# The prompt taken in by pairs of tiles between the weights' loads, and the first norm's squares made from its rows as diagonals

## The chip, the cores and the metric

One NeuronCore of a Trainium2 chip. The metric is device time in microseconds of one execution; given is the median of several runs. PE is the matrix engine (TensorE), ACT the scalar engine, DVE the vector engine, POOL the GpSimd engine, SP the sync engine, which here does nothing but issue DMAs.

## What is computed

One inference step of one decoder layer, for a prompt of 256 tokens and 8 sampled tokens that share the weights, in f32. Cut to what matters here:

```
x = x + 1/2 * SwiGLU_1(RMSNorm(x))       d_model 2048, d_ff 5632
x = x + mixer(RMSNorm(x))                dilated attention and gated linear attention
x = x + 1/2 * SwiGLU_2(RMSNorm(x))
RMSNorm(x) = x * rsqrt(mean(x * x) + 1e-6) * gain
swiglu(h)  = (silu(a) * b) @ w_out,  (a, b) = split(h @ w_in)
```

## The kernel before

**Layout.** `x` lies in SBUF with the features on the partitions: 16 tiles of 128 features x 264 tokens (256 of the prompt, 8 samples). The prompt comes from memory with tokens on the partitions (`xn`, two halves of 128 tokens x 2048 features) and is turned by PE, 128x128 at a time, against the identity matrix `ident` into PSUM (`g0`, `g1`, four banks each, `groups`), from where ACT or DVE copies it to `x`.

**Precision.** Every f32 product is made as three products of rounded parts. Of a chunk of weights (`raw`, 2 row tiles x 512 columns, 512 KB, a ring of 4 slots) ACT makes the high part `wh` (`split`, L1035) and then DVE the low part `wl` (`low`, L1458). In the same way ACT makes `xh` from x times the gain (`x_high_only`, L1051) and DVE makes `xl` (`x_low`, L1492). `multiply` (L592 to L594) issues xh*wh, xl*wh, xh*wl: 24 matmuls of 264 columns for one chunk. DVE's `low` counts `lo_done`, on which SP's next load into the slot and PE wait; PE counts `used`, on which ACT's split of the chunk four later waits.

**The first half-step.** `ffn_in` makes blocks of 512 columns of `w_in`: 8 chunks for the gate (a, in `g0`), 8 for the up part (b, in `g1`). Each engine has its own program, written out by hand, and works it off in order. The norm's factor goes on after the product: beside chunks 0 to 7 the sums of squares are made. ACT squares four tiles of x at a time (L1095), DVE adds these (L1483, L1485) into `ssq`; ahead of chunk 6 PE sums `ssq` over the partitions against ones (`mean`, L603, L604); ACT takes the root after its split of chunk 10 (k = 7, L1056), DVE its reciprocal, and chunk 8 on PE waits for the root.

**What sets the order around the change.** At the start SP issues prompt columns 0 to 511, the sample, columns 512 to 1023, waits for all six gains, and then alternates weights and prompt (`load_x`, `load_first`, L478, L452). ACT issues the loads of `ident` and of the six gains (`gain_rows`) and then waits for the first turned quarter. PE turns the prompt by quarters of four tiles (L664), with the sample (L668) and all gains (L656) between them, all of it before the first product; the third and fourth quarter wait until the banks are copied. Copies alternate: quarters 0 and 2 on ACT (L1090), 1 and 3 on DVE (L1553). Chunks 3 on of the splits are in ACT's `ffn_in` at step k (chunk k + 3), followed by `rest_of_x(k)`; DVE's program has the same steps.

Of the kernel before, what the change touches and what calls it, by code (L numbers as in the profile page):

```python
# [21 lines left out]
F32 = mybir.dt.float32  # L22
# [235 lines left out]
def layer_step(nc, x_prompt, x_sample, cache_k, cache_v, state, g_ffn1, w1_in, w1_out, g_mix, w_in,  # L258
# [5 lines left out]
    with ExitStack() as ctx:  # L264
# [113 lines left out]
        gains_in, gains_full, gains_new = sem("gains_in"), sem("gains_full"), sem("gains_new")  # L378
# [3 lines left out]
        x_in, xs_in = sems("x_in", KT // 4), sem("xs_in")  # L382
        x_turned, xs_turned, xs_new = sem("x_turned"), sem("xs_turned"), sem("xs_new")
        x_even, x_odd = sem("x_even"), sem("x_odd")
# [60 lines left out]
        def _(sp):  # L445
# [29 lines left out]
            def load_x(q):  # L475
                cols = slice(q * CW, (q + 1) * CW)
                src = x_prompt[0, :, cols].rearrange("(h p) d -> p h d", p=P)
                sp.dma_start(xn[:, :, cols], src).then_inc(x_in[q], 16)  # L478
# [102 lines left out]
        def _(pe):  # L581
# [29 lines left out]
            def ffn_in(nth, c0):  # L611
                def body(i, first):
                    for k in range(FI_BODY):
# [3 lines left out]
                        if k == 0 and first:  # L617
                            if nth == 0:
                                pe.wait_ge(x_even, 2)
# [6 lines left out]
                        if k == FI_BODY // 2:  # L626
                            if first:
# [3 lines left out]
                        if first and not up and j % 2 == 0:  # L631
# [16 lines left out]

            pe.wait_ge(ident_in, 16)
            for q in range(KT // 4):  # L650
                if q >= 2:
                    pe.wait_ge((x_even, x_odd)[q % 2], 1)
                if q == 1:
                    pe.wait_ge(gains_in, 16 * 6)
                    n_g = 4 * KT + AT_T + DV // P
                    pe.transpose(g1[:, 3, 0:n_g], gain_rows[0:n_g, :], ident[0:n_g, 0:n_g]).then_inc(gains_full, 1)  # L656
                    pe.wait_ge(gains_new, 1)
                    pe.wait_ge(xs_new, 1)
                pe.wait_ge(x_in[q], 16)
                for n in range(4):  # L660
                    f = slice((4 * q + n) * P, (4 * q + n + 1) * P)
                    g = groups[q % 2]
                    for half in range(2):
                        mm = pe.transpose(g[:, n, half * P:(half + 1) * P], xn[:, half, f], ident[:, :])  # L664
                mm.then_inc(x_turned, 1)
                if q == 0:
                    pe.wait_ge(xs_in, 16)
                    pe.transpose(g1[:, 2, 0:P], xns[:, :], ident[:, :]).then_inc(xs_turned, 1)  # L668
# [356 lines left out]
        def _(act):  # L1025
# [55 lines left out]
            for g in (g_ffn1[0], g_mix[0], g_ffn2[0], g_final, g_att[0], g_gla[0]):  # L1081
                k = g.shape[0] // P
                act.dma_start(gain_rows[n:n + k, :], g.rearrange("(k p) -> k p", p=P)).then_inc(gains_in, 16)
                n += k
            act.wait_ge(gains_new, 1)
            act.wait_ge(eps_set, 1)

            def copy_x(q):
                act.wait_ge(x_turned, q + 1)
                act.activation(x[:, 4 * q:4 * q + 4, 0:TP], groups[q % 2][:, :, 0:TP], ACT.Copy).then_inc(x_even, 1)  # L1090

            def square(q):
                if q:
                    act.wait_ge(sq_part, q)
# [971 lines left out]
```

## Time and profile before

| | us |
|---|---|
| median of 3 runs | 2084.91 (2084.04 to 2087.27) |
| the profiled execution | 2088.0 |
| its span, first to last instruction | 2086.2 |
| PE busy in the span | 2057.1 (99%) |
| DVE, ACT, POOL busy | 1149.4, 893.0, 133.4 |

The span is what the timeline shows; the execution's own time is 1.8 us longer. Times in rows count from the span's start. "Idle before" is the time in which the engine did nothing ahead of a row, with what released it. [...]

### The profile page before, as it was taken

How to read it: one execution, taken by the hardware profiler on the slowest of the kernel's cores; microseconds unless marked ns; L12 is line 12 of the kernel's file. 1: busy time of each engine (PE TensorE's matmuls, PEld its weight loads, DVE VectorE, ACT ScalarE, POOL GpSimd, SP SyncE). 2: the span in 40 equal slices, each digit the busy share in tenths (PEclk: the TensorE clock that was granted, in tenths of full speed). 3: DMA queues.
4: the chain of work that ended last, by engine and by line, in shares of the span. 5: the costliest groups of instructions: out<-in, count | busy, mean ns of one | idle time of the engine just before them, and what ended most of it. 6: DMA issues, size and time to landing. Idle time of an engine off the chain costs nothing.

```text
span 2086.2 us, 40425 instructions
## 1 busy us (share of the span) xinstructions
PE 2057.1 (99%) x16619; PEld 2034.6 (98%) x16619; DVE 1149.4 (55%) x1243; ACT 893.0 (43%) x1050; POOL 133.4 (6%) x161
## 2 busy tenths in 40 slices
PE   8999999999999999999999999999999999999998
PEld 7999999999999999999998899999999999999998
DVE  6555555555444444664578867655555555544443
ACT  6443433444344344444446734444443334433433
POOL 0000000000000001000154750000000000000000
PEclk9999999999999999999999999999999999999999
DMA  6655566656555555447987575566666665565554
GB/s 206 188 178 179 170 187 184 181 177 179 179 181 172 190 177 164 142 127 252 315 279 233 157 228 171 166 195 180 178 180 180 180 181 171 177 188 180 174 180 123
DMA packets 200857, 387.52 MB, mean 186 GB/s; under 512 B 14522, under 2 KB 23428, under 8 KB 200756
## 3 DMA queue, kind: packets, MB, share of 16 engines
q1 hardware_dynamic: 193856, 377.27, 59.2%
q10 hardware_dynamic: 6244, 7.05, 1.0%
q0 software_dynamic: 656, 1.74, 0.2%
q8 instruction: 77, 1.26, 0.2%
q14 instruction: 24, 0.20, 0.0%
HBM read 376.91 MB, written 9.11 MB: 185 GB/s over the span
## 4 chain that ended last, share of the span: by engine, by line
PE 93%; DVE 3%; ACT 1%; DMA 1%; issue 1%; POOL 0%; ACTq 0%; SPq 0%; DVEq 0%
PE g L592 30%; PE g L593 29%; PE g L594 29%; DVE wl L1458 1%; PE g L865 1%; ACT wh L1035 1%; PE g L795 0%; DVE dif L1644 0%; DVE am L1667 0%; DMA bcast<-rows_q 0%; PE g L827 0%; DMA xn<-in_x_prompt_dram 0%; POOL stream L1987 0%; PE g L816 0%; PE g L809 0%
## 5 line engine op out<-in xcount | busy, mean ns | idle before, releaser
L1458 DVE TENSOR_TENSOR wl<-raw,wh 128x1024 fp32r<-128x1024 f32 x658 | 803.3, 1231 | 775.3 <-ACT wh L1035 775.0
L1035 ACT ACTIVATE wh<-raw 128x1024 fp32r<-128x1024 f32 x658 | 689.5, 1055 | 855.0 <-PE g L594 818.4
L592 PE MATMUL g<-xh,wh 128*128 128x264 f32 x3584 | 1028.1, 287 | 5.2 <-DVE va L1611 3.6
L593 PE MATMUL g<-xl,wh 128*128 128x264 f32 x3584 | 1021.2, 285 | 0.0
L594 PE MATMUL g<-xh,wl 128*128 128x264 f32 x3584 | 1020.7, 285 | 0.0
L592 PEld LDWEIGHTS g<-xh,wh 128*128 128x128 f32 x3584 | 678.3, 189 | 10.3 <-issue 8.9
L593 PEld LDWEIGHTS g<-xl,wh 128*128 128x128 f32 x3584 | 677.1, 189 | 0.3
L594 PEld LDWEIGHTS g<-xh,wl 128*128 128x128 f32 x3584 | 675.6, 189 | 0.0
L592 PE MATMUL g<-uh,wh 128*128 128x264 f32 x1408 | 401.0, 285 | 0.0
L593 PE MATMUL g<-ul,wh 128*128 128x264 f32 x1408 | 400.6, 284 | 0.0
L594 PE MATMUL g<-uh,wl 128*128 128x264 f32 x1408 | 400.5, 284 | 0.0
L594 PEld LDWEIGHTS g<-uh,wl 128*128 128x128 f32 x1408 | 265.2, 188 | 0.0
L593 PEld LDWEIGHTS g<-ul,wh 128*128 128x128 f32 x1408 | 265.1, 188 | 0.0
L592 PEld LDWEIGHTS g<-uh,wh 128*128 128x128 f32 x1408 | 264.7, 188 | 0.0
L1074 ACT ACTIVATE uh<-t_buf 128x1056 f32 (+1 forms) x22 | 23.9, 1087 | 102.2 <-DVE t_buf L1531 102.2
L1987 POOL TENSOR_TENSOR stream<-stream,bcast 128x256 f32<-128x256 f32 x64 | 57.0, 926 | 102.4 <-DMA bcast<-rows_q 102.4
L1999 POOL TENSOR_TENSOR stream<-stream,pt_s 128x256 f32<-128x256 f32 x64 | 50.9, 830 | 38.5 <-DMA stream<-in_cache_att_v_dram 19.6
L1958 POOL DMA_DIRECT2D wg<-in_w_gate_dram x1 | 0.5, 513 | 790.6 <-PE g L594 790.6
L1535 DVE TENSOR_TENSOR ul<-t_buf,uh 128x1056 f32 (+1 forms) x22 | 27.7, 1259 | 33.2 <-ACT uh L1074 33.2
L592 PE MATMUL g<-gh,wh 128*128 128x264 f32 x128 | 38.5, 301 | 3.7 <-DVE rg L1611 3.7
L593 PE MATMUL g<-gl,wh 128*128 128x264 f32 x128 | 37.5, 293 | 0.0
L594 PE MATMUL g<-gh,wl 128*128 128x264 f32 x128 | 37.5, 293 | 0.0
(255 smaller groups left out, 1099.5 us busy)
## 6 DMA issues: line engine op xcount, KB each, us to landing
raw<-in_w_ffn_in_dram SPq DMA_DIRECT2D x352, 512.0 KB, 4.5
raw<-in_w_ffn_out_dram SPq DMA_DIRECT2D x176, 512.0 KB, 3.8
raw<-in_w_in_dram SPq DMA_DIRECT2D x96, 512.0 KB, 4.1
raw<-in_w_out_dram SPq DMA_DIRECT2D x32, 512.0 KB, 5.0
stream<-in_state_gla_dram SPq DMA_DIRECT2D x8, 512.0 KB, 7.6
bcast<-rows_v SPq DMA_DIRECT2D x8, 512.0 KB, 8.2
out_dram<-stream ACTq DMA_DIRECT2D x8, 512.0 KB, 7.7
stream<-in_cache_att_k_dram SPq DMA_DIRECT2D x8, 512.0 KB, 6.1
```

What stands on the lines that cost most here:

```text
L592: pe.matmul(out(n), hi, a, start=first and k == 0, stop=False)
L593: pe.matmul(out(n), hi, b, start=False, stop=False)
L594: mm = pe.matmul(out(n), lo, a, start=False, stop=last and k == CK_T - 1)
L865: mm = pe.matmul(held["out"][:, f, b:b + 1], stream[:, (2 * b) % 4, f * P:(f + 1) * P], ones[:, 0, :], start=True, stop=True, skip_group_c ...
L1035: act.activation(dst, src, ACT.Copy).then_inc(hi_done, 1)
L1074: act.activation(uh[:, bass.ds(4 * i, 4), :], t_buf[:, :, :], ACT.Copy).then_inc(uh_new, 1)
L1458: dve.tensor_tensor(dst, src, h.bitcast(F32), ALU.subtract).then_inc(lo_done, 1)
L1535: dve.tensor_tensor(ul[:, bass.ds(4 * i, 4), :], t_buf[:, :, :], uh[:, bass.ds(4 * i, 4), :].bitcast(F32), ALU.subtract).then_inc(ul_new, 1)
L1958: pool.dma_start(wg2[0:RANK, :], w_gate2[0]).then_inc(wg2_in, 16)
L1987: a = pool.tensor_tensor(stream[:, slot, cols], stream[:, slot, cols], bcast[:, b % 2, cols], ALU.mult)
L1999: a = pool.tensor_tensor(v[:, hs, :], v[:, hs, :], pt_s[:, t, hs, b:b + 1].to_broadcast([P, 4, HD]), ALU.mult)
```

## The change

The prompt comes in five loads (two of two tiles, three of four), each between two loads of weights, and the wait for the gains is gone from SP. PE turns it in eight pairs of tiles, all in `g1`: two before the first product, the others ahead of chunks 1, 2 and 4 (`in_front_of`). The copies from PSUM are by pairs (0, 1, 2, 4 and 6 on ACT, 3, 5 and 7 on DVE), and high and low parts are made by pairs. ACT issues a small Copy ahead of all data. The first gains (`gain_in`) are turned alone, the others ahead of chunk 5. The squares are now made from the prompt's rows: ACT squares half a row of tokens (128 tokens x 1024 features) with its accumulator, four times (`square_rows`); DVE adds the two halves and writes them, as a diagonal (`ident` times a column), into `ssq`, makes the sample's squares itself and copies the second gains (`diagonal_squares`, step k = 5).

```diff
+            def load_x(i):
+                cols = slice((0, 2, 4, 8, 12)[i] * P, (2, 4, 8, 12, 16)[i] * P)
...
             load_x(0)
             sp.dma_start(xns[:, :], x_sample[:, 0, :].rearrange("b (k c) -> k b c", c=P)).then_inc(xs_in, 16)
+            load_first(0)
             load_x(1)
-            sp.wait_ge(gains_in, 16 * 6)
-            load_first(0)
+            load_first(1)
             load_x(2)
-            load_first(1)
+            load_first(2)
             load_x(3)
-            load_first(2)
             load_first(3)
+            load_x(4)
...
+                        if first and nth == 0:
+                            in_front_of(k)
+                            if not up:
+                                pe.wait_ge(xl_pair, k + 1)
                         if first and k == 6:
                             if nth == 0:
-                                pe.wait_ge(x_odd, 2)
+                                pe.wait_ge(gains_new, 2)
                             else:
                                 pe.wait_ge(att_taken, FO_BLOCKS)
                             mean(1 + 2 * nth, mean_full)
...
+            def turn_x(pair):
+                pe.wait_ge(x_in[(0, 1, 2, 2, 3, 3, 4, 4)[pair]], 16)
+                if pair >= 4:
+                    pe.wait_ge(x_copied[pair - 4], 1)
+                for i in range(2):
+                    f = slice((2 * pair + i) * P, (2 * pair + i + 1) * P)
+                    for half in range(2):
+                        mm = pe.transpose(g1[:, pair % 4, (2 * i + half) * P:(2 * i + half + 1) * P],
+                                          xn[:, half, f], ident[:, :])
+                mm.then_inc(x_turned, 1)
...
+            turn_x(0)
+            pe.wait_ge(xs_in, 16)
+            pe.transpose(g0[:, 0, 0:P], xns[:, :], ident[:, :]).then_inc(xs_turned, 1)
+            pe.wait_ge(gain_in, 16)
+            pe.transpose(g0[:, 1, 0:KT], gain_rows[0:KT, :], ident[0:KT, 0:KT]).then_inc(gains_full, 1)
+            turn_x(1)
+            pe.wait_ge(xs_new, 1)
+            pe.wait_ge(gains_new, 1)
+
+            def in_front_of(k):
+
+                if k == 1:
+                    turn_x(2)
+                    turn_x(3)
+                elif k == 2:
+                    turn_x(4)
+                    turn_x(5)
+                elif k == 4:
+                    turn_x(6)
+                    turn_x(7)
+                elif k == 5:
+                    pe.wait_ge(gains_in, 16 * 5)
+                    pe.wait_ge(x_copied[4], 1)
...
+            act.wait_ge(eps_set, 1)
+            act.activation(tiny[:, 8:9], eps[:, 0:1], ACT.Copy)
...
+            def square_rows(n):
+                part, half = n // 2, n % 2
+                for i in ((0, 1, 2), (3, 4))[part]:
+                    act.wait_ge(x_in[i], 16)
+                if n:
+                    act.wait_ge(row_sq, n)
+                act.activation(s_buf[:, :, :].rearrange("p n t -> p (n t)")[:, 0:D // 2],
+                               xn[:, half, part * (D // 2):(part + 1) * (D // 2)], ACT.Square,
+                               accum_out=tiny[:, n:n + 1]).then_inc(row_sq, 1)
...
             def rest_of_x(k):
-                if k == 0:
-                    act.wait_ge(x_odd, 2)
-                    x_high_only(3, 0)
-                elif k <= 2:
-                    square(k + 1)
+                if k <= 4:
+                    if k % 2:
+                        copy_x(k + 3)
+                    high_pair(k + 3)
+                    if k:
+                        square_rows(k - 1)
...
+            def diagonal_squares():
+
+                dve.wait_ge(row_sq, 4)
+                link(dve.tensor_tensor(tiny[:, 4:6], tiny[:, 0:2], tiny[:, 2:4], ALU.add))
+                for half in range(2):
+                    dve.tensor_scalar(ssq[:, 0, half * P:(half + 1) * P], ident[:, :], tiny[:, 4 + half:5 + half],
+                                      None, ALU.mult)
...
             def rest_of_x(k):
+                if k <= 4:
+                    if k % 2 == 0:
+                        copy_x(k + 3)
+                    low_pair(k + 3)
+                elif k == 5:
+                    diagonal_squares()
+                    dve.wait_ge(gains_full, 2)
+                    dve.tensor_copy(all_gains[:, KT:], g1[:, 0, KT:4 * KT + AT_T + DV // P]).then_inc(gains_new, 1)
```

PE, around the mean, before (semaphores waited for in brackets; `xl_new`, `xl_pair` are low parts of x):

```order
L593 MATMUL g<-xl,wh 128x264
L594 MATMUL g<-xh,wl 128x264
L603 MATMUL g<-ssq,ones 128x264 [waits consts_in,ssq_new,x_odd]
L604 MATMUL g<-ssq,ones 128x264
L592 MATMUL g<-xh,wh 128x264 [waits lo_done,xl_new]
```

and the same place in the change:

```order
L594 MATMUL g<-xl,wh 128x264
L595 MATMUL g<-xh,wl 128x264
L604 MATMUL g<-ssq,ones 128x264 [waits ssq_new,consts_in,gains_new,xl_pair]
L605 MATMUL g<-ssq,ones 128x264
L593 MATMUL g<-xh,wh 128x264 [waits lo_done]
```

The mean stands where it stood, ahead of chunk 6; it now waits for the second gains (`gains_new`) and the low parts of pair 6 as well.

ACT, from the split of chunk 3 on, before (`used` is PE's count of chunks, `raw_full` a landed load):

```order
L1035 ACTIVATE wh<-raw 128x1024 [waits used,raw_full3]
L1051 ACTIVATE xh<-x,all_gains 128x264 [waits x_odd]
L1051 ACTIVATE xh<-x,all_gains 128x264 x3
L1035 ACTIVATE wh<-raw 128x1024 [waits used,raw_full0]
L1095 ACTIVATE s_buf<-x 128x1056 [waits sq_part]
L1035 ACTIVATE wh<-raw 128x1024 [waits used,raw_full1]
L1095 ACTIVATE s_buf<-x 128x1056 [waits sq_part]
L1035 ACTIVATE wh<-raw 128x1024 [waits used,raw_full2]
```

and the change, from the split of chunk 4 on:

```order
L1057 ACTIVATE wh<-raw 128x1024 [waits used,raw_full0]
L1113 ACTIVATE x<-g 128x2x256 [waits x_turned]
L1120 ACTIVATE xh<-x,all_gains 128x264 [waits x_copied4]
L1120 ACTIVATE xh<-x,all_gains 128x264
L1129 ACTIVATE s_buf,tiny<-xn 128x1024 [waits x_in2,x_in1,x_in0]
L1057 ACTIVATE wh<-raw 128x1024 [waits used,raw_full1]
L1120 ACTIVATE xh<-x,all_gains 128x264 [waits x_copied5]
L1120 ACTIVATE xh<-x,all_gains 128x264
L1129 ACTIVATE s_buf,tiny<-xn 128x1024 [waits x_in2,row_sq,x_in1,x_in0]
L1057 ACTIVATE wh<-raw 128x1024 [waits used,raw_full2]
```

High parts, copies and squares now stand between the splits of chunks 4 to 8, where before there were one pass of squares after chunk 4, one after chunk 5, and nothing after that.

DVE, at the end of that stretch (steps k = 4 and 5), in the change:

```order
L1496 TENSOR_TENSOR wl<-raw,wh 128x1024 [waits hi_done]
L1591 COPY x<-g 128x2x256 [waits x_turned]
L1597 SCALAR_TENSOR_TENSOR xl<-x,all_gains,xh 128x264 [waits xh_pair]
L1597 SCALAR_TENSOR_TENSOR xl<-x,all_gains,xh 128x264
L1496 TENSOR_TENSOR wl<-raw,wh 128x1024 [waits hi_done]
L1604 TENSOR_TENSOR tiny<-tiny 128x2 [waits row_sq]
L1606 TENSOR_SCALAR ssq<-ident,tiny 128x128 [waits vec]
L1606 TENSOR_SCALAR ssq<-ident,tiny 128x128
L1609 TENSOR_TENSOR t_buf<-x 128x128
L1611 TENSOR_REDUCE ssq<-t_buf 128x8 [waits vec]
L1630 COPY all_gains<-g 128x58 [waits gains_full]
```

Before, DVE's additions of squares were done by step k = 2; now `ssq` is written after the low part of chunk 8 (the second row with `wl`), and the copy of the gains comes last.

## Rows read from the trace of the kernel before

**Rows 1.** The page's chain that ended last, by engine, share of the span.
```profile
PE 93%; DVE 3%; ACT 1%; DMA 1%; issue 1%; POOL 0%; ACTq 0%; SPq 0%; DVEq 0%
```

**Rows 2.** Who PE waited for, whole span: us in total, times, longest us.
```profile
PE g L664 <- DMA xn<-in_x_prompt_dram: 9.0, 3, 5.0
PE g L592 <- DVE rg L1611: 4.9, 2, 3.7
PE g L592 <- DVE va L1611: 3.6, 1, 3.6
```

**Rows 3.** Timeline of DMA issues of SP and ACT: start us, length us, what, count.
```profile
1.99 0.58 SPq L478 DMA_DIRECT2D xn<-in_x_prompt_dram  x1
7.48 0.37 SPq L452 DMA_DIRECT2D raw<-in_w_ffn_in_dram  x1
...
3.79 0.24 ACTq L1083 DMA_DIRECT2D gain_rows<-in_g_gla_out_dram  x1
```

**Rows 4.** Timeline of PE, 3 to 45 us, same columns, then [idle before].
```profile
5.01 1.94 PE L664 MATMUL g<-ident,xn 128*128 128x128 f32 x8 [5.01 <-DMA xn<-in_x_prompt_dram]
...
16.14 1.94 PE L664 MATMUL g<-ident,xn 128*128 128x128 f32 x8 [0.71 <-DMA xn<-in_x_prompt_dram]
17.73 0.57 PE L592 MATMUL g<-xh,wh 128*128 128x264 f32 x1
...
20.30 0.33 PE L594 MATMUL g<-xh,wl 128*128 128x264 f32 x1
...
36.54 0.61 PE L603 MATMUL g<-ssq,ones 128*128 128x264 f32 x2
...
43.53 0.39 PE L592 MATMUL g<-xh,wh 128*128 128x264 f32 x1
```

**Rows 5.** Timeline of ACT, 0 to 60 us, same columns.
```profile
7.06 1.28 ACT L1090 ACT_TABLE_LOAD   x1 [7.06 <-PE g L664]
...
9.41 1.73 ACT L1051 ACTIVATE xh<-x,all_gains 128x264 fp32r<-128x264 f32 x4
11.30 1.06 ACT L1035 ACTIVATE wh<-raw 128x1024 fp32r<-128x1024 f32 x1 [0.16 <-DMA raw<-in_w_ffn_in_dram]
...
19.15 1.04 ACT L1035 ACTIVATE wh<-raw 128x1024 fp32r<-128x1024 f32 x1
...
52.65 1.06 ACT L1035 ACTIVATE wh<-raw 128x1024 fp32r<-128x1024 f32 x1 [1.85 <-PE g L594]
55.57 1.06 ACT L1035 ACTIVATE wh<-raw 128x1024 fp32r<-128x1024 f32 x1 [1.86 <-PE g L594]
```

**Rows 6.** Timeline of DVE, 19 to 38 us, same columns.
```profile
19.26 1.70 DVE L1492 SCALAR_TENSOR_TENSOR xl<-x,all_gains,xh 128x264 fp32r<-128x264 f32 x4
20.88 0.70 DVE L1483 TENSOR_TENSOR t_buf<-s_buf 128x528 f32<-128x528 f32 x1
...
34.10 3.49 DVE L1458 TENSOR_TENSOR wl<-raw,wh 128x1024 fp32r<-128x1024 f32 x3
```

**Rows 7.** Groups by line and form: count, busy us, mean ns, idle us.
```profile
L1203 ACT ACTIVATE cum<-g 128x512 f32<-128x512 f32 x2 | 1.2, 598 | 5.8 <-PE g L729 5.8
...
L1263 ACT ACTIVATION_READ_ACCUMULATOR sm<-sm,tiny 128x1 f32 x16 | 3.0, 189 | 0.0
...
L1629 DVE SCALAR_TENSOR_TENSOR la<-g,dif 128x512 f32<-128x512 f32 x2 | 1.3, 686 | 8.1 <-ACT dif L1196 8.1
...
L1769 DVE TENSOR_SCALAR prod<-ident,sm_s 128x128 f32<-128x128 f32 x1 | 0.3, 286 | 0.0
```

**Rows 8.** PE by stretches: us, busy (count), granted clock, DMA share, GB/s.
```profile
1042.00:1044.00 2.00, 1.39 (x6) 0.50 1.03 363
1046.00:1048.00 2.00, 2.00 (x12) 0.56 1.02 371
...
1188.00:1190.00 2.00, 1.43 (x6) 0.50 0.00 0
...
1194.00:1196.00 2.00, 2.00 (x18) 0.86 0.00 0
```

More of the change, by code:

```diff
@@ L626, in body @@
                         if k == FI_BODY // 2:
+                            if first and nth == 0:
+                                for pair in range(4, 8):
+                                    pe.wait_ge(x_copied[pair], 1)
                             if first:
@@ L630, in body @@
                                 pe.wait_ge(up_in, i + FI_BLOCKS * nth)
-                        if first and not up and j % 2 == 0:
+                        if first and nth and not up and j % 2 == 0:
                             pe.wait_ge(xl_new, 8 * nth + j // 2 + 1)
@@ L1092, in square, with copy_x @@
-            def square(q):
-                if q:
-                    act.wait_ge(sq_part, q)
-                act.activation(s_buf[:, :, :], x[:, 4 * q:4 * q + 4, :], ACT.Square).then_inc(sq_new, 1)
-            copy_x(0)
-            act.wait_ge(x_even, 1)
-            act.wait_ge(xs_new, 1)
-            x_high_only(0, 0)
+            act.wait_ge(eps_set, 1)
+            act.activation(tiny[:, 8:9], eps[:, 0:1], ACT.Copy)
+            def copy_x(pair):
+                act.wait_ge(x_turned, pair + 1)
+                act.activation(x[:, 2 * pair:2 * pair + 2, 0:TP],
+                               g1[:, pair % 4, :].rearrange("p (n t) -> p n t", n=2),
+                               ACT.Copy).then_inc(x_copied[pair], 1)
@@ new lines, in high_pair @@
+            def high_pair(pair):
+                act.wait_ge(x_copied[pair], 1)
+                for n in (2 * pair, 2 * pair + 1):
+                    a = act.activation(xh[:, n, :], x[:, n, :], ACT.Copy, scale=gains[:, 0, n:n + 1])
+                a.then_inc(xh_pair, 1)
+            def square_rows(n):
[7 more added lines that the diff above has]
+                               accum_out=tiny[:, n:n + 1]).then_inc(row_sq, 1)
@@ L1548, in _, with copy_x @@
             dve.wait_ge(gains_new, 1)
-            clear_squares()
-            def copy_x(q):
-                dve.wait_ge(x_turned, q + 1)
-                dve.tensor_copy(x[:, 4 * q:4 * q + 4, 0:TP], groups[q % 2][:, :, 0:TP]).then_inc(x_odd, 1)
-            copy_x(1)
-            x_low(0, 0, 0, sums=False)
+            def copy_x(pair):
+                dve.wait_ge(x_turned, pair + 1)
+                dve.tensor_copy(x[:, 2 * pair:2 * pair + 2, 0:TP],
+                                g1[:, pair % 4, :].rearrange("p (n t) -> p n t", n=2)).then_inc(x_copied[pair], 1)
@@ new lines, in low_pair @@
+            def low_pair(pair):
+                dve.wait_ge(xh_pair, pair + 1)
+                for n in (2 * pair, 2 * pair + 1):
+                    a = dve.scalar_tensor_tensor(out=xl[:, n, :], in0=x[:, n, :], scalar=gains[:, 0, n:n + 1],
+                                                 in1=xh[:, n, :].bitcast(F32), op0=ALU.mult, op1=ALU.subtract)
+                a.then_inc(xl_pair, 1)
+            def diagonal_squares():
[4 more added lines that the diff above has]
+                                      None, ALU.mult)
+                sq = t_buf[:, 0, 0:P]
+                link(dve.tensor_tensor(sq.rearrange("p (k b) -> p k b", b=TS), x[:, :, TP:T], x[:, :, TP:T],
+                                       ALU.mult))
+                dve.tensor_reduce(ssq[:, 0, TP:T], sq.rearrange("p (k b) -> p b k", b=TS), AX_X,
+                                  ALU.add).then_inc(ssq_new, 4)
```

79 lines of the change are left out of this document (27 added, 52 removed).

## The prediction

> **What bounds the kernel now.** I read the page first. The chain that ended last is 93% PE [rows 1], so almost anything off PE is free once the weights flow, and only work ahead of the first long run of products can be won. The list of PE's waits then says where PE stands still: 9.0 us for the prompt in three waits, and two places in the mixer of 3.7 and 3.6 us which the change doesn't touch [rows 2]. So only the first 45 us matter, and I went through them engine by engine. Three instants carry the sum: the first product starts at 17.73, the matmuls of the mean start at 36.54, and chunk 8 (the first of the "up" half, which waits for the square root) starts at 43.53 [rows 4]. From there on the order of both kernels is the same and PE-bound: ACT's splits start 2.92 us apart, each after 1.85 us of waiting for PE [rows 5]. **The change in the time is therefore the change in the start of chunk 8.** I call chunk c the 24 products (each 264 columns wide) made with weight chunk c, 0.12 us apart, 2.92 us in all.
>
> **Part 1: the start.** Before, SP issues the third load at 1.99 and then waits for the gains until 7.48 [rows 3]. The wait goes, and the first chunk of weights takes that third place. On an empty queue such a load landed 3.8 us after its issue (7.48 to 11.30, [rows 3, 5]); behind the first quarter of the prompt and the sample I put it at 6.3. Of the prompt's first two tiles I take 4.3, since twice that much had landed by 5.01 [rows 4]. ACT ends its DMA issues at 4.03 [rows 3]; the table load of 1.28 [rows 5], which stood behind data, now runs there, and ACT is free at 5.5. Its copy of two tiles from PSUM is 0.60 (`cum`, the same shape, [rows 7]), to 6.1. The high parts then need the sample copied and the first gains, each a load, a turn and a DVE copy: 6.5. A pair of tiles is 0.82 until the next can start (four took 1.73, [rows 5]), the split takes 1.05, DVE's low part 1.2 (three in 3.49, [rows 6]). That makes 6.5 + 0.8 + 1.1 + 1.3 = **9.7 for the first product, 8.0 us earlier than before**. The bounds: the gains might land as late as the last ones did before (7.4, the end of the wait just named), which gives 11.6; nothing can come before 9.1, as ACT and DVE alone need that from 5.5 on.
>
> **Part 2: chunk 0 to 5 on PE.** In rows 4 PE's products start 0.22 us apart, the 1.2 GHz level, up to 20.30 and 0.12 after it; the rise comes 4.2 us after the unbroken stretch began with the last transposes at 16.14. I carry this over: of chunk 0, 19 products at 0.22 and 5 at 0.12, 4.9 us, end at 14.6. The same rows allow another reading: counted from the first product alone, 17.73, the rise comes after 2.6 us; then chunk 0 has 12 products at each pace, 4.1 us, and everything below comes 0.8 us sooner. One rise fits both; I take the first, since PE's transposes stand in the trace as full matmuls and I see nothing there that sets them apart. [...] After chunk 0 PE turns two pairs (0.9 us at 2.4 GHz, half of the 1.94 in [rows 4]) ahead of chunks 1, 2 and 4. So far PE would run: chunk 1 from 15.5, chunk 2 from 19.3, chunk 3 from 22.7, chunk 4 from 26.5, chunk 5 from 30.1 to **33.0**; 0.5 us of waiting for low parts stands before chunk 3 and again before chunk 5 (from the schedule of part 3).
>
> **Part 3: what ACT and DVE must do meanwhile.** This is where I look for the price. Before, ACT's own work was ahead of PE's need; now PE turns pairs 2 and 3 only behind chunk 0, and ACT's copy of pair 2 stands in its queue until 15.3. From there both queues run by themselves. Pair 2: copy 0.64, high 0.82, split 2 0.95, split 3 1.05, to 18.8. DVE's low part of chunk 3 follows its chunk 2, up to 20.1, and only then comes its copy of pair 3, 0.7 (between 0.60 of ACT's and 0.69 of a DVE operation of 128x512 from PSUM, [rows 7]); ACT has waited for that and has its high parts done at 21.7. Then come four steps of ffn_in:
> - a step in which ACT copies (k = 1, 3): split 0.95 + copy 0.64 + high 0.82 + squares of 1024 elements with the accumulator read 1.15 (about 0.95 as a split of the same size, [rows 5], and 0.19, [rows 7]) = 3.56;
> - a step in which DVE copies (k = 2, 4): ACT's split must end (1.09), DVE's low part goes first (1.14), then its copy (0.72), then ACT's high parts (0.82) and squares (1.15) = 4.92.
>
> Together 2 x (3.56 + 4.92) = 17.0, to 38.6. Against this PE needs 2.92 per chunk. In step k = 5 DVE waits for split 8 (1.09) and makes its low part (1.14), and only then the new sums: an addition of two columns 0.2, two diagonals 0.29 each (the same operation on `ident` took 286 ns, [rows 7]), the sample's product and its reduction 0.6, the other gains 0.2: 1.6. **The sum is ready at 42.5.** What it replaces (four squares over x, eight additions of 0.7, [rows 6]) lay beside PE's work and ended before 34.1, when DVE makes nothing but low parts [rows 6], so taking it away frees nothing.
>
> **Part 4: the wait.** PE asks for the mean ahead of chunk 6, as before, now with the second gains, and chunks 6 and 7 stand in its queue behind that wait; ACT's split 10 waits for chunk 6 and the root for the split, so nothing goes round it. PE stands from 33.0 to 42.5, 9.5 us, and starts the mean 5.9 us later than before (36.54). Then the clock: after the two mixer gaps of 3.6 and 3.7 us [rows 2] the granted clock is 0.50 until 1047.8 and 1194.6, that is 5.1 and 6.0 us after work came back [rows 8] (the windows hold 1.39 and 1.43 us of work, so it came at 1042.61 and 1188.57). The rise at the program's start took 4.2. I take 4.7 us at half speed: 2.35 us lost. Two transposes of gains instead of one cost 0.1, in the above.
>
> **Sum:** 5.9 + 2.35 = 8.2, less 0.1 as the short wait for the root before chunk 8 is partly covered: **+8.1 us**. The profiled execution (span 2086.2, 2088.0 in all) would become 2096.1; it lies 3.1 over the median of the three runs, 2084.91, to which I add the same: **2093.0**. Loads after the fourth chunk aren't in the sum: they wait for low parts as before and are issued well over 3.8 us before the split that needs them.
>
> **The rivals.**
> - *Transposes don't count for the clock* (part 2's other reading, as a mechanism of this kernel: the rise 2.6 us after the first product). 2092.2. For and against stand above: 0.17. [...]
> - *The start is later*: gains or weights land late, the first product at 11.6. Then +10, 2095. The start of a queue is the least known part; but the small loads are first in theirs: 0.09.
> - *The wait, but no cold clock behind it*: 5.9, so 2090.8. Both mixer gaps speak against: 0.05.
> - *Not slower: PE stays the bound.* If ACT and DVE overlapped better than my two queues do (DVE's copies not holding ACT's high parts, the sums ready by 32.0), PE would drop its 1.0 us of small waits and the 9.5, start the mean at 32.0 and chunk 8 at 38.9: 4.6 us sooner, 2080.3. It decides at this point: the sum ready before 36.5 if the clock stays up, before 34.1 if it falls. For it: ACT's busy time in those steps (3.56 of each) is near PE's 2.92 plus turns; against: both queues are strictly in order in the listing, and three copies of DVE stand behind a low part that itself waits for ACT. 8.4 us would have to be wrong: 0.10.
> - *It doesn't do what it says*: had the mean's operands nothing to do with the new squares, this would be as the last one; the listing shows the wait, so it has no chance of its own.
>
> **How the numbers follow.** The forecast itself has 0.55, with an own range of +6 to +10: ACT and DVE steps each off by 0.1 to 0.2 us (ten of them), the clock's 4.2 to 6.0. Left is 0.04 for a middle course, in which the waits are half as long. A measurement of this kernel can tell 0.2%, 4.2 us. Slower by more: 0.55 + 0.17 + 0.09 and nearly all of the 0.05, less what small errors in the steps take off, 0.81. Faster by more: most of the 0.10, as 4.6 is just over 4.2: 0.07. Within: 0.12. The range leaves out the gain (0.10) and some 0.07 at its ends: 2087.5 to 2096.5.
>
> **What would show it.** First product at 9 to 10.5; PE idle for about 9 us before the first matmul of the mean, with "DVE all_gains" as the releaser; that matmul at 41 to 44; a granted clock of 0.5 for some 5 us after it; chunk 8 at about 51.6; in ACT's timeline, high parts of pairs 3, 5 and 7 each with about 2 us of idle before them. I am wrong if the mean starts before 38, if PE waits for the prompt or the weights between chunks 1 and 5, or if later stages give some of the 8 us back.

## The result, and the profile after

| | before | with the change |
|---|---|---|
| median of 7 runs, us | 2085.23 (2083.93 to 2087.27) | 2092.92 (2090.30 to 2095.48) |
| ratio | | 1.0036, 95% interval 1.0027 to 1.0045 |
| profiled execution, its span | 2088.0, 2086.2 | 2091.84, 2090.0 |
| first product | 17.73 | 9.68 |
| first matmul of the mean | 36.54 | 42.78 |
| first product of chunk 8 | 43.53 | 51.81 |

The change costs 5.6 to 9.4 us (the interval times 2085). The two profiled executions lie only 3.8 us apart, because the one of before was slower than any of the seven runs and the one of the change the second fastest of its seven; what goes with this is told below. Up to chunk 8 they can be compared directly.

PE's timeline of the changed kernel (start us, length us, what, [idle before]), the counterpart of [rows 4]:

```profile
4.10 1.08 PE L661 MATMUL g<-ident,xn 128*128 128x128 f32 x4 [4.10 <-DMA xn<-in_x_prompt_dram]
...
9.68 0.56 PE L593 MATMUL g<-xh,wh 128*128 128x264 f32 x1 [0.59 <-DVE wl L1496]
...
14.87 0.42 PE L595 MATMUL g<-xh,wl 128*128 128x264 f32 x1
15.09 1.41 PE L661 MATMUL g<-ident,xn 128*128 128x128 f32 x8
...
42.78 1.22 PE L604 MATMUL g<-ssq,ones 128*128 128x264 f32 x2 [8.84 <-DVE all_gains L1630]
```

A later stretch of the same view:

```profile
51.81 0.36 PE L593 MATMUL g<-xh,wh 128*128 128x264 f32 x1 [0.28 <-ACT root L1078]
```

The first product comes 8.05 us earlier, the mean 6.24 us later: PE stands still for 8.84 us, and its releaser is the last operation of step k = 5, DVE's copy of the second gains. ACT's timeline, the counterpart of [rows 5], shows where the time goes:

```profile
16.10 0.60 ACT L1113 ACTIVATE x<-g 128x512 f32<-128x512 f32 x1 [4.48 <-PE g L661]
...
21.64 0.92 ACT L1120 ACTIVATE xh<-x,all_gains 128x264 fp32r<-128x264 f32 x2 [2.09 <-DVE x L1591]
22.46 1.04 ACT L1057 ACTIVATE wh<-raw 128x1024 fp32r<-128x1024 f32 x1
...
25.89 1.05 ACT L1057 ACTIVATE wh<-raw 128x1024 fp32r<-128x1024 f32 x1
28.83 0.92 ACT L1120 ACTIVATE xh<-x,all_gains 128x264 fp32r<-128x264 f32 x2 [1.89 <-DVE x L1591]
...
30.71 1.04 ACT L1057 ACTIVATE wh<-raw 128x1024 fp32r<-128x1024 f32 x1
...
34.13 1.04 ACT L1057 ACTIVATE wh<-raw 128x1024 fp32r<-128x1024 f32 x1
37.06 0.92 ACT L1120 ACTIVATE xh<-x,all_gains 128x264 fp32r<-128x264 f32 x2 [1.89 <-DVE x L1591]
37.89 1.04 ACT L1129 ACTIVATE s_buf<-xn 128x1024 f32<-128x1024 f32 x1
38.84 0.18 ACT L1129 ACTIVATION_READ_ACCUMULATOR s_buf<-xn 128x1 f32 x1
38.93 1.99 ACT L1057 ACTIVATE wh<-raw 128x1024 fp32r<-128x1024 f32 x2
```

These are the splits (L1057) of chunks 4 to 8 at 22.46, 25.89, 30.71, 34.13 and 38.93: two steps of 3.4 us and two of 4.8, where [rows 5] had one of 2.92 that waited for PE. None of these waits for PE any more, and the high parts of pairs 3, 5 and 7 stand 1.9 to 2.1 us behind DVE's copy. Then DVE's end of the chain:

```profile
40.00 1.23 DVE L1496 TENSOR_TENSOR wl<-raw,wh 128x1024 fp32r<-128x1024 f32 x1 [1.09 <-ACT wh L1057]
41.14 0.15 DVE L1604 TENSOR_TENSOR tiny<-tiny 128x2 f32<-128x2 f32 x1
41.33 0.48 DVE L1606 TENSOR_SCALAR ssq<-ident,tiny 128x128 f32<-128x128 f32 x2
41.73 0.28 DVE L1609 TENSOR_TENSOR t_buf<-x 128x128 f32<-128x128 f32 x1
42.12 0.38 DVE L1611 TENSOR_REDUCE ssq<-t_buf 128x8 f32<-128x128 f32 x1
42.41 0.21 DVE L1630 COPY all_gains<-g 128x58 f32<-128x58 f32 x1
```

And PE by stretches (us, busy (count), granted clock as a share of the full one, DMA share, GB/s), with the clock down in the wait and for a while after it. Within 44:46, at 0.50, the products start 0.22 us apart, within 48:50, at 1.00, 0.12: these two paces are the half and the full clock of what follows. The row of one product is 0.42 us long at the first pace and 0.28 at the second, more than the distance to the next, so the pace is read from the starts. At the very start this view reads 1.00 although the products start 0.22 us apart (10:12, for instance), so in the first stretch the clock is told by the distance between starts.

```profile
32.00:34.00 2.00, 1.94 (x16) 1.00 0.00 0
34.00:36.00 2.00, 0.00 (x0) 1.00 0.91 255
36.00:38.00 2.00, 0.00 (x0) 0.58 0.29 37
...
44.00:46.00 2.00, 2.00 (x9) 0.50 0.64 167
46.00:48.00 2.00, 2.00 (x16) 0.86 0.38 141
48.00:50.00 2.00, 2.00 (x19) 1.00 0.00 0
```

**After chunk 8.** PE's waits over the whole span, the counterpart of [rows 2]:

```profile
PE g L604 <- DVE all_gains L1630: 8.8, 1, 8.8
PE g L661 <- DMA xn<-in_x_prompt_dram: 6.5, 2, 4.1
PE g L593 <- DVE rg L1670: 4.9, 2, 3.7
...
PE g L593 <- DVE va L1670: 1.5, 1, 1.5
```

The wait for `va` in the mixer is 1.5 us here and was 3.6, and the granted clock was down for 6.8 us in the whole rest of this execution, for 17.1 us in that of before. The table under the experiments has one profiled execution of each kernel and so can't part the kernel from the execution. But the 80 runs of the kernel before, taken beside the experiments, spread by 6 us by themselves (2083.25 to 2089.32), and their mean time is 2084.4 where the mean granted clock was 0.997, 2085.2 at 0.996 and 2085.9 at 0.995.

### The profile page after: what moved, and what is told of

Its sections match the earlier page's. It is cut to its first block, busy times and chain, and to the rows that moved or that the text cites. A ratio compares the mean times of both kernels' runs of the same rounds, so it can differ in the third digit from the quotient of the medians.

```text
span 2090.0 us, 40450 instructions
## 1 busy us (share of the span) xinstructions
PE 2055.4 (98%) x16620; PEld 2032.1 (97%) x16620; DVE 1146.9 (55%) x1242; ACT 894.6 (43%) x1058; POOL 134.3 (6%) x161
## 4 chain that ended last, share of the span: by engine, by line
PE 91%; DVE 4%; ACT 3%; issue 1%; DMA 1%; POOL 0%; SPq 0%; ACTq 0%; DVEq 0%
PE g L593 29%; PE g L594 29%; PE g L595 29%; DVE wl L1496 1%; ACT wh L1057 1%; PE g L887 0%; PE g L817 0%; DVE dif L1703 0%; DVE am L1726 0%; PE g L849 0%; POOL stream L2046 0%; DMA bcast<-rows_q 0%; PE g L831 0%; PE g L838 0%; PE g L830 0%
## 5 line engine op out<-in xcount | busy, mean ns | idle before, releaser
L1057 ACT ACTIVATE wh<-raw 128x1024 fp32r<-128x1024 f32 x658 | 689.5, 1055 | 856.1 <-PE g L595 812.6
L2058 POOL TENSOR_TENSOR stream<-stream,pt_s 128x256 f32<-128x256 f32 x64 | 52.6, 857 | 37.5 <-ACT prod L1335 19.0
```

The costliest lines, as they stand in the source:

```text
L1057: act.activation(dst, src, ACT.Copy).then_inc(hi_done, 1)
L2058: a = pool.tensor_tensor(v[:, hs, :], v[:, hs, :], pt_s[:, t, hs, b:b + 1].to_broadcast([P, 4, HD]), ALU.mult)
```

## The experiments

The theory: the sums of squares come at the end of a chain in the two queues of ACT and DVE, which starts with ACT's copy of pair 2 and ends with DVE's copy of the second gains 26.5 us later (26.7 to the mean on PE); PE asks for them ahead of chunk 6, and its clock falls while it waits. The rivals: the pairs' work as such costs; an early start is always given back; the form of the squares costs; the clock costs nothing.

All times below are of one profiled execution each; "rest" is its span from chunk 8 on, "clock down" the time with a granted clock of 0.5 from the mixer to the end of the last product.

| kernel | first product | mean | chunk 8 | rest | clock down in the rest | median of runs |
|---|---|---|---|---|---|---|
| before | 17.73 | 36.54 | 43.53 | 2042.7 | 17.1 | 2084.7 to 2085.2 |
| the change | 9.68 | 42.78 | 51.81 | 2038.2 | 6.8 | 2092.92 |
| mean_late | 10.43 | 42.87 | 44.80 | 2039.9 | 10.2 | 2085.68 |
| dve_copy_first | 10.30 | 37.14 | 46.36 | 2040.5 | 13.7 | 2086.50 |
| keep_busy | 10.37 | 42.07 | 49.25 | 2039.5 | 10.2 | 2092.08 |
| one_square | 9.91 | 38.18 | 47.74 | 2037.5 | 6.8 | 2087.06 (one) |
| loads_only | 17.92 | 37.07 | 44.06 | 2038.2 | 6.8 | 2084.70 |
| turn_early | 10.23 | 39.52 | 48.78 | 2040.5 | 13.7 | 2091.08 (one) |
| squares_only | 17.69 | 36.83 | 44.17 | 2037.9 | 6.8 | 2085.95 |
| all_gains_first | 12.85 | 45.62 | 54.54 | 2043.5 | 17.1 | 2099.80 (one) |
| three | 10.30 | 37.41 | 39.23 | 2039.8 | 10.2 | 2080.88 |
| three_mean7 | 10.42 | 36.12 | 39.92 | 2038.4 | 10.2 | 2080.19 |
| fill_turns | 10.14 | 34.25 | 38.12 | 2039.1 | 10.2 | 2079.47 |
| fill_products | 10.51 | 34.74 | 38.61 | 2039.2 | 10.2 | 2079.10 |

The rest sorts itself by the time with the clock down: 2037.5 to 2038.2 with it down for 6.8 us, 2038.4 to 2039.9 with 10.2, 2040.5 with 13.7, 2042.7 and 2043.5 with 17.1. From 6.8 to 17.1 us it grows by 4.5 to 6.0 us, about half of the 10.3 us more at the half clock, where products start 0.22 us apart and not 0.12. So single executions of two kernels can differ by 6 us for what happens behind the edit, and the start of chunk 8 says better what the edit does. That start has a scatter of its own: up to the first product the change and seven of the other kernels (mean_late, dve_copy_first, keep_busy, one_square, turn_early, three, three_mean7) are the same, yet it comes between 9.68 and 10.43, and the clock rises 2.1 to 6.2 us after it.

**mean_late: the mean where PE can afford to wait.**

```diff
-                        if first and k == 6:
+                        if first and k == (8 if nth == 0 else 6):
```

> The mean and its wait for the sums and the second gains stand ahead of chunk 8 instead of chunk 6; nothing else is changed. If the wait for the sums is what costs (my theory), chunks 6 and 7 fill it: chunk 7 waits for the low parts of pair 7 until 38.9 and ends at 41.9, the mean starts at 42.8 as in the changed kernel, chunk 8 at about 44.4 with the clock up (43.53 before, 51.81 with the change), and the run takes +0.9 us against before, some 2086. If the clock falls in the small gaps, up to 47 and +3.5. The rival, that the eight microseconds come from the pairs' work as a whole (transposes between chunks, squares, small loads) and not from where PE waits, expects chunk 8 above 50 and over +6 us.

Measured: the mean at 42.87, where it was; chunk 8 at 44.80, 7.0 us sooner than in the change; the ratio to before 1.0003 (0.9993 to 1.0013). The sums came no sooner, only PE didn't stand in front of them, and no other part of the pairs' work was touched. The rival that the pairs' work as such costs the eight microseconds falls. PE's timeline has one wait for a low part of pair 7 and then the mean at the full clock (its two halves start 0.55 us apart, in the change 1.01):

```profile
39.16 0.39 PE L593 MATMUL g<-xh,wh 128*128 128x264 f32 x1 [1.58 <-DVE xl L1597]
...
42.87 0.71 PE L604 MATMUL g<-ssq,ones 128*128 128x264 f32 x2 [0.54 <-DVE all_gains L1630]
43.42 0.61 PE L605 MATMUL g<-ssq,ones 128*128 128x264 f32 x2
44.80 0.36 PE L593 MATMUL g<-xh,wh 128*128 128x264 f32 x1 [0.77 <-ACT root L1078]
```

**dve_copy_first: the chain shortened.**

```diff
+                        if first and nth == 0 and k in (0, 2, 4):
+                            copy_x(k + 3)
                         low(FI_BODY * i + (c0 + k + 3), (c0 + k + 3) % RING)
...
                 if k <= 4:
-                    if k % 2 == 0:
-                        copy_x(k + 3)
                     low_pair(k + 3)
```

> DVE copies pairs 3, 5 and 7 ahead of the low part of its step instead of behind it, so ACT doesn't stand 1.9 to 2.1 us before the high parts of these pairs. My theory (two queues in order, which hold each other up three times) expects the sums ready 5.9 us earlier: the mean at 36.9 instead of 42.8, chunk 8 at 43.9 to 46.4 by the clock after a wait of some 3.5 us, the run at +0.4 to +3 us against before. The rival, that ACT's amount of work alone sets the pace, expects the mean no more than 2 us earlier and more than +5 us.

Measured: the mean at 37.14; from ACT's copy of pair 2 (15.60) to there 21.5 us instead of 26.7, 5.1 less of the 5.9 forecast. PE's wait of 4.7 us remained and the clock fell all the same (granted 0.50 from 38 to 40, 9.2 us from the mean to chunk 8), so chunk 8 is at 46.36, the upper end of what was expected. The ratio is 1.0004 (0.9995 to 1.0014). Three waits of two engines for each other were thus worth 5 of the 6.2 us by which the mean is late; the rival of ACT's amount of work alone, which allowed 2 us, falls.

**keep_busy: the clock by itself.**

```diff
                             if nth == 0:
+                                pe.wait_ge(x_copied[5], 1)
+                                for _ in range(72):
+                                    pe.matmul(g1[:, 1, 0:T], xh[:, 0, 0:P], xh[:, 1, :], start=True, stop=True)
                                 pe.wait_ge(gains_new, 2)
```

> 72 products that nothing uses (into a free PSUM bank) stand on PE ahead of the wait for the sums, 8.8 us of work in the 8.84 us of idle time. The theory of the clock: the mean starts at 42.8 as before but at 2.4 GHz, chunk 8 at 49.9 instead of 51.81, the run 1.9 us faster than the change, so +6 us against before. If the cold clock costs nothing there (all of it is the wait), chunk 8 stays at 51.8.

Measured: from the mean to chunk 8 7.18 us instead of 9.03, 1.85 less. The granted clock stays at 1.00 there. The run, 2092.08, can't be told from the change's 2092.92: of the 1.9 us forecast it shows 0.8, within the noise. The 72 products filled PE from 33.17 to the mean at 42.07:

```profile
33.17 9.06 PE L626 MATMUL g<-xh 128*128 128x264 f32 x72 [0.24 <-DVE xl L1600]
42.07 0.61 PE L604 MATMUL g<-ssq,ones 128*128 128x264 f32 x2
49.25 0.36 PE L593 MATMUL g<-xh,wh 128*128 128x264 f32 x1 [0.28 <-ACT root L1081]
```

DVE was done with the sums and the gains at 41.66 here, since the chain's head lay at 15.11, so the filling held the mean up by 0.4 us. Chunk 8 comes 2.6 us sooner than in the change; 1.85 of this is the clock, the rest the earlier head.

**one_square: what ACT's queue weighs.** Three of the four squarings are left out, so the sums are not those of the reference.

```diff
-                    if k:
+                    if k == 1:
                         square_rows(k - 1)
...
-                dve.wait_ge(row_sq, 4)
+                dve.wait_ge(row_sq, 1)
```

> Three of ACT's four squarings of the prompt's rows are left out, so the sums and all that is scaled by them are not those of the reference. If ACT's queue up to the sums is the critical chain, the mean starts 3 x 1.14 = 3.4 us earlier, at 39.4, and chunk 8 at about 48.3; if the sums waited for something else (DVE's steps, a transfer), the mean moves by less than 1 us.

Measured: the mean at 38.18, 4.6 us sooner, more than the 3.4 expected. The surplus is not the squares': the copy of pair 2 starts at 14.64 instead of 16.10, since PE's clock rose at 12.4 (the starts of the products are 0.22 us apart up to 12.25 and 0.12 from 12.44 on), in the middle of chunk 0, and not after it. From that copy to the mean it is 23.5 us instead of 26.7: 3.1 for three squarings. The same distance is 26.6 in mean_late and 26.7 in turn_early, so the chain is one of a fixed length, and what shifts its head shifts the mean.

**loads_only: the first part of the change alone, on the kernel before.**

```diff
+            load_first(0)
             load_x(1)
-            sp.wait_ge(gains_in, 16 * 6)
-            load_first(0)
-            load_x(2)
             load_first(1)
+            load_x(2)
```

> The kernel before with one part of the change: SP doesn't wait for the gains and alternates weights and prompt (first quarter, sample, weights 0, second quarter, weights 1, third quarter, weights 2, fourth quarter, weights 3). All other engines are as before. My theory (the start is won by the loads, the loss comes from the pairs' queues and the late sums) expects no wait for the third and fourth quarter on PE: the third is turned from 9.4 (behind ACT's copy), the fourth from 11.6 (behind DVE's copy), and the first product at about 14.3 instead of 17.73, behind ACT's copy of the third quarter and the first low part; nothing later waits, so the run takes -3.3 us against before, some 2081.8. The rival, that an earlier start is always given back, expects the mean at 36.5 as before and no change.

This missed. The first product comes at 17.92, and the ratio is 1.0002 (0.9993 to 1.0011). The place is in PE's timeline:

```profile
5.18 1.94 PE L663 MATMUL g<-ident,xn 128*128 128x128 f32 x8 [5.18 <-DMA xn<-in_x_prompt_dram]
11.01 0.38 PE L655 MATMUL g<-ident,gain_rows 74*128 74x74 f32 x1 [3.68 <-DMA gain_rows<-in_g_gla_out_dram]
11.72 4.51 PE L663 MATMUL g<-ident,xn 128*128 128x128 f32 x24 [0.33 <-DVE all_gains L1546]
17.92 0.36 PE L591 MATMUL g<-xh,wh 128*128 128x264 f32 x1 [1.69 <-DVE wl L1457]
```

The edit is not quite what was expected of it: the fourth quarter of the prompt is issued ahead of weights 2 and not behind them. What that alone does was not measured. The prompt was there (24 turns follow in one piece), but the last of the small loads of gains, issued by ACT at 3.79 as before, landed at 11.0 instead of 7.46. Between 6 and 8 us the DMA engines moved 362 and 331 GB/s here, and in the kernel before 74 and then nothing. So SP's wait, which looked like idle time, had kept the large loads out of the way of the small ones. Removed alone it gives nothing: what it lets in early is under way while PE waits 3.68 us for the gains.

The same trace shows one thing more. The next product starts 0.20 us after the first, the one behind it 0.12:

```profile
18.12 0.28 PE L592 MATMUL g<-xl,wh 128*128 128x264 f32 x1
18.24 0.28 PE L593 MATMUL g<-xh,wl 128*128 128x264 f32 x1
```

So PE was at the full clock before it had made any product. It had made nothing but turns, and the 24 took 4.51 us where at 0.22 us each they would have taken 5.3: the clock rose among them. In the kernel before, half of chunk 0 (12 products, up to 20.30) still stood 0.22 us apart. The 1.2 us that this saves is lost again in two waits for low parts of weights (1.1 us), which the kernel before doesn't have: chunk 8 comes at 44.06.

**all_gains_first: is it the split of the gains that carries the start?**

```diff
             pe.wait_ge(gain_in, 16)
+            pe.wait_ge(gains_in, 16 * 5)
```

> The change, but PE waits for all six gains ahead of turning the first ones, as before. In the kernel with the loads alone the six gains had landed only at 11.0 (7.46 before), beside the large loads that no wait holds back any more. If that holds here, the first gains are turned at 11 instead of 5.33, the high parts of pair 0 come at 11.6 instead of 6.15 and the first product at 15.1 instead of 9.68; all that follows moves by 5 us, chunk 8 to 56 to 57, the run to +13 us against before. If the small loads are not slowed here, they are there at 7.5 and chunk 8 comes by 53.5.

Measured: the gains are turned at 9.02, the first product is at 12.85 and chunk 8 at 54.54. The small loads are late here too, by 1.6 us and not by the 3.5 of loads_only, so what follows moves by 2.7 to 3.2 us, half of what I expected. Turning the first gains alone is worth 3.2 us of the start, or 2.4 to 2.9 if the seven other kernels with the change's start are compared (9.91 to 10.43). What the other parts of the change give of its 8 us was not taken apart. The one run took 2099.80, of which 2043.5 lie behind chunk 8, the longest rest of all, so it says little. How late such a load gets differs by 2 us between these two executions; I have two values and no rule.

**squares_only: the other part alone, on the kernel before.**

```diff
-                act.activation(s_buf[:, :, :], x[:, 4 * q:4 * q + 4, :], ACT.Square).then_inc(sq_new, 1)
+                act.activation(s_buf[:, :, :].rearrange("p n t -> p (n t)")[:, 0:D // 2],
+                               xn[:, half, part * (D // 2):(part + 1) * (D // 2)], ACT.Square,
+                               accum_out=tiny[:, n:n + 1]).then_inc(sq_new, 1)
...
-                elif k <= 2:
-                    add_squares(k + 1)
-                    if k == 2:
-                        dve.sem_inc(x_new, 4)
+                elif k == 2:
+                    diagonal_squares()
+                    dve.sem_inc(sq_part, 4)
+                    dve.sem_inc(x_new, 4)
```

> The kernel before with the other part of the change alone: the four squarings are those of the prompt's rows with the accumulator, at the same places in ACT's program, and DVE makes the diagonals at step k = 2. The theory that only the place of the sums costs (behind step k = 5 of queues that the pairs fill) expects nothing from their form: first product at 17.7, sums ready before 34, mean at 36.5, chunk 8 at 43.5, within 1 us of before in the trace up to there and within 0.1% in the run. If the form costs (the accumulator reads, ACT's reading of the rows), chunk 8 moves by 2 us or more.

Measured: the mean at 36.83, chunk 8 at 44.17 (0.6 later, of which 0.4 is a wait for the root), the ratio 1.0004 (0.9995 to 1.0013). The diagonals are made from 29.75 on and wait for nothing; their form costs nothing that can be told from noise. In the change it is their place that costs.

**turn_early: the head of the chain.**

```diff
-                            in_front_of(k)
+                            if k == 5:
+                                in_front_of(k)
...
-                                 final_read if k == 0 and first and nth else None)
+                                 final_read if k == 0 and first and nth else
+                                 (lambda n, k=k: in_front_of(k + 1) if n == 1 else None)
+                                 if first and nth == 0 and k in (0, 1, 3) else None)
```

> The change with the turns of pairs 2 to 7 put inside the chunk ahead (behind its first 6 products) instead of behind it. My theory puts the head of the chain at ACT's copy of pair 2 (16.10), which waits for chunk 0 to end: the copy comes at 12.3, the sums 3.7 us earlier, the mean at 39.1, chunk 8 at about 48.2. If the head of the chain is elsewhere (a load), the mean stays above 42.

Measured: ACT's copy of pair 2 at 12.78, the mean at 39.52, chunk 8 at 48.78, each within 0.6 us of what was expected. The chain does start there, and it is as long as before (26.7).

**three and three_mean7: the edits together.** `three` is mean_late, dve_copy_first and turn_early in one; `three_mean7` differs in one number:

```diff
-                        if first and k == (8 if nth == 0 else 6):
+                        if first and k == (7 if nth == 0 else 6):
```

> The change with the three edits together: turns inside the chunk ahead, DVE's copies ahead of the low part, the mean ahead of chunk 8. The waits add up to 5.6 + 3.7 us less for the sums, which are ready at about 33.5, before PE ends chunk 7 (39.4, its own work from the first product on at 9.7 to 10.4); chunk 8 waits for the mean and the root, and starts at 40.9 to 41.6, -2 to -2.6 us against before: 2082.5 to 2083. If ACT's amount of work sets the pace, chunk 8 starts at 43 to 45 and the run is no faster than before.

> As the kernel with three edits, but with the mean ahead of chunk 7: chunk 7 covers the root, so chunk 8 starts 0.6 us sooner, at 40.3 to 41, if the sums are there when chunk 6 ends (36.5), -2.6 to -3.2 us against before. If they are later than that, it is no better than the mean ahead of chunk 8.

Measured: chunk 8 at 39.23 and 39.92, 4.3 and 3.6 us sooner than before, 1.7 and 0.4 us ahead of the earlier ends of what was expected, although the sums were ready only at 34.65 and 34.52 (33.5 expected); ratios 0.9981 (0.9972 to 0.9990) and 0.9977 (0.9967 to 0.9986). **Both are faster than the kernel before, by 0.2%, and than the change**, and the rival that an early start is always given back falls. Between the two the runs don't decide (2080.88 and 2080.19), nor do the traces: the clock rose 2.1 us after the first product in `three` and 5.4 us after it in `three_mean7`, which by itself is 1.6 us of chunk 8's start (half of the difference, an estimate). In `three_mean7` the mean waits for nothing:

```profile
36.12 0.61 PE L604 MATMUL g<-ssq,ones 128*128 128x264 f32 x2
36.57 0.61 PE L605 MATMUL g<-ssq,ones 128*128 128x264 f32 x2
```

**fill_turns and fill_products: what lifts the clock.** On `three_mean7`, PE's waits ahead of chunk 0 are filled, with turns or with products of the identity matrix (here the turns; 6 and 2 products in their place):

```diff
+            for _ in range(13):
+                pe.transpose(g0[:, 3, 0:P], ident[:, :], ident[:, :])
             turn_x(1)
+            for _ in range(4):
+                pe.transpose(g0[:, 3, 0:P], ident[:, :], ident[:, :])
```

> The kernel with the three edits and the mean ahead of chunk 7 (2080.19), with 17 turns of the identity matrix, which nothing uses, in PE's waits ahead of chunk 0 (13 for the second load of the prompt, 4 for the first low part), so that PE turns without a break of 0.5 us or more from 4.2 to the first product at about 10.4. If turns count for the clock as the prediction took it, chunk 0 runs at 0.12 us a product from its start or from 1 us on, and chunk 8 comes 2 to 2.5 us sooner than 39.9. [...]

> The same with 8 plain f32 products of the identity matrix in place of the 17 turns, some 3.5 us of work. Both readings expect the clock up by the first product or within 2 us of it, and chunk 8 at 37.5 to 38.5; if neither this nor the turns move it, something else than PE's own work sets the rise.

PE's timeline of fill_turns:

```profile
5.60 3.04 PE L675 MATMUL g<-ident 128*128 128x128 f32 x13
8.52 1.11 PE L664 MATMUL g<-ident,xn 128*128 128x128 f32 x4
9.43 1.01 PE L678 MATMUL g<-ident 128*128 128x128 f32 x4
10.14 0.42 PE L593 MATMUL g<-xh,wh 128*128 128x264 f32 x1
10.39 0.28 PE L594 MATMUL g<-xl,wh 128*128 128x264 f32 x1
10.51 0.28 PE L595 MATMUL g<-xh,wl 128*128 128x264 f32 x1
```

Nothing but turns ran before, and the second product already starts 0.12 us ahead of the third: the full clock from the second product on. In `three_mean7` the products were still 0.22 us apart at 15.34, 4.9 us after the first. The mean comes at 34.25 instead of 36.12, of which 0.3 is an earlier first product. Chunk 8 comes at 38.12, 1.8 us sooner, where 2 to 2.5 were expected (the mean now waits 0.4 us for the sums); with products in place of the turns it comes at 38.61, just outside the 37.5 to 38.5 expected. Part of the 1.8 is the late rise in the one execution of `three_mean7`, 5.4 us after the first product. Products do the same as turns (34.74, with a first product 0.4 later). By the second reading, in which only products count, chunk 8 would have stayed near 39.9; for these f32 turns, which the trace lists as plain matmuls against the identity, this run and loads_only (its second and third product start 0.12 us apart) say otherwise. Ratios 0.9975 (0.9965 to 0.9985) and 0.9972 (0.9962 to 0.9982); the gain over three_mean7, 0.7 and 1.1 us of the medians, is less than the runs can tell, and only the trace shows it.

## Why the prediction was right, point by point

- **The start** (9.7 for the first product): 9.68. That this is exact is luck: in the seven other kernels that are the same up to there it came at 9.91 to 10.43. Its parts were less exact than the sum. ACT's first copy came at 5.45 (5.5), the high parts at 6.15 (6.5), since the gains were there sooner; the weights took until 7.2 (6.3), and the split started at 7.21.
- **Chunk 0** (4.9 us, clock up 4.2 us after the first product): mis-sized. Its products stood 0.22 us apart to its end, and it took 5.4 us (9.68 to 15.09). The rise after 4.2 us, and the 2.6 of the second reading, were both taken from one rise, as if the delay were fixed. It isn't: with the same start it came 2.1 us after the first product in three, 2.5 in one_square, 5.0 in mean_late, 5.4 in three_mean7 and 6.2 in the change, among the turns behind chunk 0. The head of the chain was therefore at 16.10 instead of 15.3; in the others with their turns at the same place it was at 14.64 to 16.29. So neither reading held as a number, and 0.8 us of the forecast was left to chance. The reason given for the second, that turns don't count, is refuted by loads_only and fill_turns, though the result itself could not have shown it. No run shows the 1.2 and 2.4 GHz that the prediction here, and the expectation of keep_busy, put to the two paces: the traces show products 0.22 and 0.12 us apart and granted clocks of 0.50 and 1.00. The 0.9 us taken for the turns of two pairs at the full clock was 0.78 (19.27 to 20.05).
- **The steps of ACT and DVE** (3.56 and 4.92 us): 3.43 and 4.82, 3.42 and 4.80; over four steps 16.5 us instead of 17.0. The sum ready at 42.5: 42.6. Here errors of opposite sign cancelled: 0.8 us too little at the head, 0.5 too much in the steps and 0.2 too much in the last part (3.7 us instead of 3.9). Two additions in the prediction are off by 0.1 us (21.7 and 17.0 give 38.7, the last part 42.4), and its terms for chunk 0 give 4.8 and not 4.9; none of this matters.
- **The wait** (9.5 us): 8.84, since chunk 5 ended at 33.9 and not at 33.0; 0.75 us of this is there at the start of chunk 1 (16.25 and not 15.5), by the colder chunk 0. The mean 5.9 us later than before: 6.24.
- **The cold clock** (2.35 us): the clock came back at about 46.6, 3.8 us after the mean began, and not 4.7; from the mean to chunk 8 it is 9.03 us, before 6.99: 2.04. keep_busy, which takes it away, gets 1.85. The rival without this cost falls.
- **Chunk 8** (+8.1): +8.28, and the medians differ by 7.7. The forecast of 2093.0 lay 0.1 us from the median; as the interval for the difference is 5.6 to 9.4 us, that closeness is luck as well, and the trace's 8.28 says more.
- **"PE stays the bound"**, the rival of the other side: as a description of the changed kernel wrong, since the queues hold each other up as listed. As a mechanism it is real: with the three edits PE stays the bound, and the gain is near the one computed: 4.6 us there, 3.6 to 4.3 in the traces and 3.8 to 4.5 in the medians.
- **"It takes nothing away that mattered"** (the old squares): squares_only confirms it.
- **The start as a gain by itself** was not put in question in the prediction beyond a late load, and it should have been. The wait for the gains was read as idle time only; loads_only shows that it also kept large loads away from small ones (the last gains turned at 11.01 and not at 7.50). In the change the split of the gains hides this (all_gains_first).

## What to carry to other kernels

A start that comes earlier is worth what the next fixed point on the bounding engine lets through (here no gain with the mean ahead of chunk 6, where chunk 8 came 8.28 us later, and 3.6 to 4.3 us with the three edits): look for the first operation there that needs the end of another queue, and either move it back as far as its result allows (here from chunk 6 to chunk 7 or 8, one number) or shorten that queue. Where two in-order engines hand work to and fro, put what the other one waits for ahead of what only comes from it; three such swaps were worth 5 us. And judge an edit of a few microseconds by a fixed event in the timeline, not by the end of one execution, when the time with the clock down elsewhere in the program differs from execution to execution (here 6.8 to 17.1 us).

## What the runs showed that I had not expected

- The small loads on ACT's queue came later where SP's large loads ran beside them: PE turned the last gains at 7.50 and 7.29 with SP waiting (before, squares_only), at 11.0 and 9.0 without (loads_only, all_gains_first). These are four executions; how much later is not known as a rule.
- The rest of the program from chunk 8 on takes 2037.5 to 2043.5 us, in step with how long the granted clock is down in it (6.8 to 17.1 us). Why it is down for longer in one execution than in another stays open. The wait for `va` in front of it was between 1.0 and 4.1 us.
- Turns of f32 tiles lifted PE's clock as products did: with nothing but turns before, products two and three start 0.12 us apart in loads_only and fill_turns; with products in place of the filling turns it is 0.13 (fill_products), and without filling 0.22 (three_mean7).
- How long after the first product the clock rises is not fixed: 2.1 to 6.2 us in eight executions with the same start.
